# Gate tiles turned instead of selection tiles, and the last pair's down weights in eight pieces

## The reference, cut to what matters

```python
def block_ffn(args):            # one block of rows that belongs to one expert
    tok, e = args
    xb = xt[tok]
    hb = jax.nn.silu(xb @ w1[e]) * (xb @ w3[e])
    return hb @ w2[e]
...
y = jnp.einsum('nk,nkd->nd', gate.astype(xt.dtype), y_assign)   # gate-weighted sum over a token's two experts
```

## Time and profile before

| | |
|---|---|
| time, median of 3 runs | 1326.96 us (1324.94 to 1327.0) |
| the profiled execution: its time, its span | 1323.78 us, 1322.1 us |
| PE, DVE, ACT busy | 1289.8 us (98%), 695.4 us (53%), 501.6 us (38%) |
| DMA over the span | 363.68 MB, mean 275 GB/s |
| the 16 pairs of experts | from about 428 to 883 us of the span |

### The profile page before, as it was taken

The page is one execution under the profiler, slowest core; times in us unless marked ns, Lnnn a source line. Parts: engine busy times, 40 slices in busy tenths (PEclk is TensorE's granted clock), DMA queues, the critical chain, the costliest instruction groups (busy, mean ns, idle before and its releaser), DMA issues.

```text
span 1322.1 us, 18062 instructions
## 1 busy us (share of the span) xinstructions
PE 1289.8 (98%) x7214; PEld 908.7 (69%) x7214; DVE 695.4 (53%) x1174; ACT 501.6 (38%) x766; POOL 77.3 (6%) x83
## 2 busy tenths in 40 slices
PE   8999999999999999999999999999999999999998
PEld 7988887976775445444445444459956687799986
DVE  5675668666565222222322222257876877755552
ACT  5555574345242211111111111146414685744442
POOL 5740200100000000000000000000000000000000
PEclk9999999999999999999999999999999999999999
DMA  9653747958865999999999999995505334655540
GB/s 350 229 191 135 254 144 260 368 194 303 308 232 199 396 424 427 427 427 428 428 428 428 427 425 428 427 397 181 180 12 196 139 129 157 195 166 183 192 159 32
DMA packets 101349, 363.68 MB, mean 275 GB/s; under 512 B 4002, under 2 KB 28837, under 8 KB 88912
## 3 DMA queue, kind: packets, MB, share of 16 engines
q1 hardware_dynamic: 97792, 352.86, 68.7%
q0 software_dynamic: 3280, 9.58, 2.2%
q10 hardware_dynamic: 192, 0.06, 0.0%
HBM read 361.43 MB, written 1.05 MB: 274 GB/s over the span
## 4 chain that ended last, share of the span: by engine, by line
PE 84%; DVE 7%; ACT 4%; DMA 2%; issue 2%; ACTq 0%; DVEq 0%
PE bank L510 37%; PE bank L908 15%; PE bank L926 9%; PE bank L883 5%; PE bank L1253 5%; PE bank L939 2%; DVE ring_parts L1301 2%; DMA ring<-in_w 2%; PE bank L835 1%; PE bank L1056 1%; PE bank L916 1%; ACT ring_parts L2119 1%; PE bank L564 1%; DMA ring<-in_w_xkv 1%; PE bank L600 1%
## 5 line engine op out<-in xcount | busy, mean ns | idle before, releaser
L2119 ACT ACTIVATE ring_parts<-ring 128x1024 fp32r<-128x1024 f32 x234 | 242.6, 1057 | 231.5 <-PE bank L510 204.2
L1301 DVE TENSOR_TENSOR ring_parts<-ring,ring_parts 128x1024 fp32r<-128x1024 f32 x214 | 257.3, 1223 | 133.1 <-ACT ring_parts L2119 130.1
L510 PE MATMUL bank<-ring_parts,arena_parts 128*128 128x512 f32 x1056 | 271.7, 392 | 3.6 <-ACT ring_parts L2119 1.5
L510 PEld LDWEIGHTS bank<-ring_parts,arena_parts 128*128 128x128 f32 x1056 | 196.4, 188 | 48.7 <-ACT ring_parts L2119 2.9
L510 PE MATMUL bank<-arena_parts,ring_parts 128*128 128x256 f32 x1504 | 198.0, 284 | 1.2 <-DVE flank_parts L1307 0.7
L909 PE MATMUL bank<-ring,arena 128*64 128x512 f32 x448 | 197.9, 594 | 0.0
L908 PE MATMUL bank<-ring,arena 128*64 128x512 f32 x432 | 190.7, 594 | 6.1 <-issue 6.1
L510 PEld LDWEIGHTS bank<-arena_parts,ring_parts 128*128 128x128 f32 x1504 | 190.1, 192 | 2.1 <-DVE flank_parts L1307 0.8
L908 PEld LDWEIGHTS bank<-ring,arena 128*64 128x64 f32 x432 | 57.4, 137 | 125.3 <-issue 125.3
L510 PE MATMUL bank<-ring_parts 128*128 128x512 f32 (+1 forms) x624 | 117.2, 346 | 2.1 <-DVE ring_parts L1301 1.2
L926 PE MATMUL bank<-ring,arena 128*64 128x512 f32 x448 | 113.4, 595 | 1.1 <-DMA ring<-in_w 1.1
(11 more groups left out here) (385 smaller groups left out, 1440.0 us busy)
## 6 DMA issues: line engine op xcount, KB each, us to landing
ring<-in_w SPq DMA_DIRECT2D x83, 2048.0 KB, 20.4
ring<-in_w_in SPq DMA_DIRECT2D x27, 2048.0 KB, 9.4
flank<-in_w SPq DMA_DIRECT2D x13, 2048.0 KB, 20.7
ring<-in_w_ada SPq DMA_DIRECT2D x12, 2048.0 KB, 8.0
ring<-in_w_ffn_gate SPq DMA_DIRECT2D x11, 1024.0 KB, 5.4
ring<-in_w_ffn_up SPq DMA_DIRECT2D x11, 1024.0 KB, 8.0
ring<-in_w_ffn_down SPq DMA_DIRECT2D x5, 2048.0 KB, 7.9
ring<-in_w_xkv SPq DMA_DIRECT2D x4, 2048.0 KB, 16.3
```

The costliest lines, as they stand in the source:

```text
L510: mm = pe.matmul(ps[:, o:o + width], *pair, start=(o == 0 and kk == 0 and ha + hw == 0), stop=(kk == kn - 1 and (ha, hw) == terms[-1] and ...
L1301: dve.tensor_tensor(low, src, high, ALU.subtract).then_inc(low_ready, 1)
L2119: act.activation(high, src, ACT.Copy).then_inc(high_ready, 1)
```

## The change

There are two parts.

1. TensorE turns `gateB` instead of `selB`, and no longer sums the gates by matmuls. Since a slot holds one token or none, each row of the turned gate tile has one number or none that isn't zero. ScalarE copies the turned tile to `gate_rest` in one instruction whose sum over the row (`accum_out`) is the slot's gate. VectorE makes the selection from it: 1 where `gate_rest` isn't 0 (`picked`, a new instruction between `acc` of the pair before and `hid`). ScalarE's `gt` no longer waits for the scatters of the pair before, since it writes no tile that they read; `picked` waits for them instead.
2. The w2 matrices of the last pair (loads 94 and 95) are issued as eight DMAs of 512 KB, block `k` of both experts with a semaphore of its own, `last_piece[k]`, and a run of 4 KB in each partition. The last down product goes block by block (`down_by_pieces`): for each `k` both halves, after a wait for that block.

```diff
@@ TensorE, slots_turned and the last pair's down product
-                    pe.transpose(PS[1][:, t * P:(t + 1) * P], selB[:, t, :], ident[:])
-                for t in range(NT):
-                    mm = pe.matmul(PS[1][:, N:N + 1], gateB[:, t, :], ones[:, 0:1], start=(t == 0), stop=(t == NT - 1))
+                    mm = pe.transpose(PS[1][:, t * P:(t + 1) * P], gateB[:, t, :], ident[:])
                 mm.then_inc(moe["gated"], 1)
...
+            def down_by_pieces(n):
+                w2u = [moe_place((WHOLE + j) % PLACES).rearrange("p (k n) -> p k n", k=KF) for j in range(2)]
+                reach(pe, moe["hid"], 2 * n + 2)
+                for half in range(2):
+                    reach(pe, moe[f"low{half}"], n)
+                for k in range(KF):
+                    pe.wait_ge(last_piece[k], 32)
+                    for half in range(2):
+                        for j in range(2):
+                            mm = pe.matmul(PS[4 + half][j * C:(j + 1) * C, :], hidT[:, j, k, :],
+                                           w2u[j][:, k, half * 512:(half + 1) * 512], start=(k == 0), stop=(k == KF - 1),
+                                           skip_group_check=True)
+                        if k == KF - 1:
+                            mm.then_inc(moe["down"], 1)
...
             def scatter(n, half):
-                reach(pe, moe["gt"], n + 1)
+                reach(pe, moe["picked"], n + 1)
...
@@ VectorE
+            def picked(n):
+                reach(dve, moe["gt"], n + 1)
+                reach(dve, moe["scattered"], 4 * n)
+                dve.tensor_scalar(selT, gate_rest, 0.0, None, ALU.not_equal).then_inc(moe["picked"], 1)
...
             def step(n, col, after, before):
                 if after:
                     acc(n - 1)
+                picked(n)
                 hid(n, 0)
...
@@ ScalarE
             def gt(n):
                 reach(act, moe["gated"], n + 1)
-                reach(act, moe["scattered"], 4 * n)
                 reach(act, moe["low1"], n)
-                act.activation(slot_gate, PS[1][:, N:N + 1], ACT.Copy)
-                act.activation(selT, PS[1][:, 0:N], ACT.Copy).then_inc(moe["gt"], 1)
+                reach(act, moe["picked"], n)
+                act.activation(gate_rest, PS[1][:, 0:N], ACT.Copy, accum_out=slot_gate).then_inc(moe["gt"], 1)
...
@@ SyncE, the loads of the experts' weights (WHOLE = UNITS * PAIRS - 2 = 94)
-                expert_load(i % PLACES, 2 * n + u // 3, u % 3)
+                if i < WHOLE:
+                    expert_load(i % PLACES, 2 * n + u // 3, u % 3)
+            for k in range(KF):
+                for j in range(2):
+                    src = w["w2"][0, NE - 2 + j].rearrange("(p k) n -> p k n", p=P)
+                    sp.dma_start(moe_place((WHOLE + j) % PLACES)[:, k * D:(k + 1) * D], src[:, k, :]).then_inc(last_piece[k], 16)
```

More of the change, by code:

```diff
@@ L241, in two_blocks @@
         slot_gate = stat[:, 0:1]
+        gate_rest = arena[:, 4864:5120]
         dft_tabs = [tiles(9216 + 512 * i, 2, N) for i in range(2)]
@@ L334, in two_blocks @@
         first_piece = [sem(f"first_piece{q}") for q in range(4)]
+        last_piece = [sem(f"last_piece{k}") for k in range(KF)]
         act_chain, dve_chain, pool_chain = sem("act_chain"), sem("dve_chain"), sem("pool_chain")
@@ L348, in moe_sems @@
             m = {n: sem(f"{tag}_{n}") for n in (
-                "sel", "gate", "gathered", "gated", "upped", "turned", "down", "scattered",
+                "sel", "gate", "gathered", "gated", "picked", "upped", "turned", "down", "scattered",
                 "xg", "gt", "h13", "sil", "hid", "y0", "y1", "low0", "low1", "acc")}
@@ L359, in two_blocks @@
         UNITS = len(ORDER)
+        WHOLE = UNITS * PAIRS - 2
         def moe_place(m):
@@ L372, in moe_unit @@
                 return at % PLACES, 16 * (at // PLACES + 1)
-            return m, 16 * (len(range(m, UNITS * PAIRS, PLACES)) - PAIRS + 1 + n)
+            return m, 16 * (len(range(m, WHOLE, PLACES)) - PAIRS + 1 + n)
         def reach(eng, which, value):
@@ L958, in step @@
                     gather(n + 1, 1)
-                down(n)
+                    down(n)
+                else:
+                    down_by_pieces(n)
                 if not after:
```

## The result

Four runs of the changed kernel took 1333.49, 1333.70, 1335.91 and 1336.26 us, a median of 1334.81. Four of the kernel before, beside them, had a median of 1326.86. The change makes the kernel slower by 7.95 us: ratio 1.0058, with a 95% interval of 1.0042 to 1.0074. The forecast was 1326.7 us in a range of 1324.0 to 1328.7, so it was wrong, and on the side that it had given a chance of 0.10.

The account below looks back on a forecast made before the run. DMA was taken to set the long-run pace, with TensorE first living on a lead. Stream and piece terms summed to -0.2 us (-0.9 to +1.1), taking 1326.96 to about 1326.7 us, range 1324.0 to 1328.7.

Parts of the forecast that it names:

- starts at about 882.85 instead of 883.07: Second block's first product: scatter and weight split were tied; now the split decides, so it starts at about 882.85 us.
- TensorE loses the two matmuls with ones: Each expert pair on TensorE: four matmul records fewer, 0.37 us a pair.
- C: Last w2 loads: slow pieces with fixed costs laid bare delay the next block's weights; +5.4 us, 1332.4; chance 0.07.
- D: Expert pairs: VectorE's new wait outlasts 4.2 us of cover and reaches TensorE; +2.7 us, 1329.7; chance 0.03.
- behind it TensorE runs without a gap for 11.17 us: After the second block's first product: TensorE runs on gapless for 11.17, 1.75, then 56.45 us, keeping the shift.
- DMA's pace: Expert pairs: loads set the long-run 29.4 us a pair; idle behind late down products grows from 0.93 to about 1.3.
- rival B: Expert pairs: all those at TensorE's pace count, eight to ten times 0.37; -3.3 us, 1323.7; chance 0.09.
- VectorE's and ScalarE's new work: Expert pairs: `picked` takes 0.35 us, reading the sum 0.2; 4.2 us of cover keeps the gather from waiting.
- The last down product: Last pair: released by `hid`, not DMA; runs 7.1 us without gaps and ends at 878.5 instead of 879.53.
- The stream of loads 0.5 us earlier: Weight loads of the experts: gaps at the stream's start shrink, the stream comes 0.5 us earlier, range 0 to 0.74.
- The other order of the blocks at nothing: End of the last down product: block-wise order delays copies and sums by 0, upper end 0.7 us.
- The 4 KB runs at 0.43 us: Last w2 pieces: 409 GB/s instead of 427 delays the next weights by 0.43 us, bounds 0 and 1.08.

Follow-up runs that it names:

- e4: The changed kernel with only the w2 pieces and block-wise down product, selection and gate sums as in the kernel before: 1327.54 us, ratio 0.9992.
- e5: The kernel before, without the branch after the experts and the skipped code for overfull experts on every engine: 1326.91 us, ratio 0.9996.
- e6: The changed kernel, without the branch after the experts and the skipped code for overfull experts on every engine: 1326.59 us, ratio 0.9992.
- e1: The changed kernel plus 128 idle waiting instructions on TensorE ahead of the branch: 1326.99 us, ratio 0.9989.
- e7: The changed kernel with two `up` calls left out of TensorE's skipped code, so the jump spans 192 instructions instead of 325: 1326.87 us, ratio 0.9994.
- e8: The kernel before plus 64 idle waiting instructions on TensorE ahead of the branch: 1327.72 us, single run.
- e12: The kernel before plus 224 idle waiting instructions on TensorE ahead of the branch: 1328.33 us, single run.
- e9: The kernel before plus 96 idle waiting instructions on TensorE ahead of the branch: 1334.11 us, single run.
- e2: The kernel before plus 128 idle waiting instructions on TensorE ahead of the branch: 1338.67 us, ratio 1.0080.
- e3: The changed kernel with only the turned gates, last w2 loads whole and the down product as before: 1336.78 us, ratio 1.0060.
- e10: The kernel before plus 160 idle waiting instructions on TensorE ahead of the branch: 1332.27 us, single run.
- e11: The kernel before plus 192 idle waiting instructions on TensorE ahead of the branch: 1339.04 us, single run.

## Why the prediction was wrong, step by step

**The step that failed.** The prediction said of the second block's first product that it "starts at about 882.85 instead of 883.07", taking that two paths end there, the last scatter and the split. In the profile after it started at 890.42. There was a third path, TensorE's own instructions, and the sum had no term for it. "TensorE loses the two matmuls with ones" was priced as 0.37 us of time in each pair; that the same edit takes 8 instructions a pair out of the program, and so moves a jump 128 instructions down, was not looked at. Of the rivals, C and D ended on the slower side, with mechanisms that the runs refute: pieces that are slow (e4), and a new wait on VectorE that reaches TensorE (see below). A time near the measured one from C or D would have been a right number for a wrong reason.

A second term failed with it: "behind it TensorE runs without a gap for 11.17 us, ... so the shift is kept". Behind a gap of 5.8 us the granted clock is at its lower level for some time, and the 48 products take 2.5 us more. A stall of TensorE is not over when it ends.

**Terms that held.** Without the jump the forecast of "no change" is what e5 against e6 and e1 against the kernel before show. By its parts:

The pair on TensorE. The down products of pairs 1 and 2 start 27.87 us apart now (chain of waits), against 28.22; the forecast was 0.37 less, measured 0.35. From the turned tile to the turned hidden tile it is 0.22 us in the last pair (862.56 to 862.78) instead of 0.58.

```profile
471.57 7.02 PE bank L927 x32
...
499.44 7.02 PE bank L927 x32
```

DMA's pace. The idle time behind the down products was to grow from 0.93 to about 1.3 us with the pairs at 29.4. It is 1.26, the pairs from 787.49 to 846.23 are 29.37 us apart, and the first wait behind a down product now comes at 646 rather than 705 us (before, one of 1.15 us stood within a pair at 685): TensorE spends its lead sooner and wins nothing (rival B is out).

```profile
646.10 1.28 issue
...
787.49 7.02 PE bank L927 x32
...
816.87 7.02 PE bank L927 x32
...
846.23 7.02 PE bank L927 x32
853.25 1.26 issue
```

VectorE's and ScalarE's new work. `picked` takes 0.28 us (forecast 0.35), the reading of the sum 0.20 (forecast 0.2), and no gather waits for either (rival D is out). The rows of the last pair:

```profile
863.96 0.20 ACT L2395 ACTIVATION_READ_ACCUMULATOR arena<-bank 128x1 f32 x1
...
865.08 0.28 DVE L1800 TENSOR_SCALAR arena_parts<-arena 128x256 fp32r<-128x256 f32 x1
865.28 0.41 DVE L1805 TENSOR_TENSOR arena<-arena,bank 128x256 f32<-128x256 f32 x1
```

The last down product. It was to be released by `hid` and not by a DMA, and to take 7.1 us without gaps: it is, at 873.82, and it took 7.09. Less the 1.7 us by which this execution was late before the experts, it starts 0.3 us earlier than before; the forecast was 1.0, of which 0.5 was to come from the stream.

**Terms that were off by little.** The stream of loads 0.5 us earlier: measured about 0, since the last pair's first scatter lies 1.77 us later than before against the 1.7 that were there already. The other order of the blocks at nothing (bounds 0 to 0.7): from the down product's end to the last scatter's end it is 3.71 us now and was 3.48, so 0.23. The 4 KB runs at 0.43 us: in the stretch that holds mostly pieces the queue moved 409 GB/s, the very rate of the forecast's row (before, 432 from 864 to 868):

```profile
DMA packets 696, 2.45 MB, mean 409 GB/s; under 512 B 75, under 2 KB 75, under 8 KB 695
```

(Window 864 to 870 us; the next load's first packets come in at 868.8.) The split starts 0.77 us later than before, so 0.95 earlier if all of the 1.7 is taken off, where the forecast had 0.07; what gave the rest isn't shown. e4's time is that of the kernel before: the pieces cost nothing that can be told from none, and rival C is out. On the page DMA: Bandwidth & Descriptors (Bandwidth) the Trainium skill has a figure for 1 MB that would have made them an estimated 2.5 us slower than now; the 409 GB/s of the trace speak against it for queued transfers.

Two slips of the working change nothing in this. "One 512 KB load alone", the row behind rival C's price, is of two loads issued one behind the other. And the upper bound of the sum should be about +0.9 and not +1.1, since the 1.08 us of slow runs would first use up the 0.2 us by which the split was ready early.

**Why it was missed.** What would have shown it was at hand: the branch stands in the quoted code between the last pair and the second block, and the profile lists 60 instruction fetches of 16 KB for a program whose length can be counted. The 0.06 us of "issue" ahead of L510 looked like proof that this place is free. It was free by its position.

## What to carry to other kernels

Where a program has a jump over much code, count instructions as well as time: an edit that only takes instructions away can move the jump to a place where its target isn't at hand, and here that cost 5.8 us of standing and up to 2.7 us of low clock, some twenty times the 0.37 us that it takes off a pair. The sign in the profile is idle time with the releaser "issue" at a branch, with an instruction fetch inside it; the fetch by itself is no sign, since it follows the jump in the good places too. Before a change is thrown away for such a loss, pad the program or shorten the skipped code and time it again: e1 and e7 brought back the 8 us.

## What the runs showed of the hardware

- TensorE's instructions came in fetches of 16 KB, one per 256 instructions of the count. A jump one block on cost nothing that shows (e8, e12, the kernel before); two blocks on cost 5.80 to 5.83 us in five kernels, whatever the place in the block.
- In the changed kernel the last scatter ended at 884.62, the fetch lies in the window 887.4 to 887.9, and the first product started at 890.42. What the 2.8 us before that window are spent on stays open. In the kernel before the next fetch also comes about 3 us after its jump (886.23 against 883.01), while TensorE works on; without a jump (e5, e6) it doesn't come.
- The jump of 325 or 333 instructions is 69 or 77 more than 256, so by the table about three places in ten of a branch are bad ones (an estimate: 69 to 77 of 256). Another 50 or so would cost a part, as e9's 3.01 us, where the products left in the target's block take less time than the 5.66 us after which its wait ended (25 products at 0.23 us, two instructions each).
- After 5.8 us of standing, the 48 products took 13.64 us (after), 12.66 (e2), 13.86 (e3), 12.51 (e10) and 13.86 (e11), against 11.17 and 11.04 to 11.17 in the other kernels with a jump and without a gap there; the granted clock was 0.50 in the changed kernel from 890.4 to 895.4 us. So the low clock cost 1.3 to 2.7 us.
